# Cache attention: key products in two 512-column halves, scores of four pages at once on four column groups

## What is computed

```python
def scores(c, kr):                                    # c (128, 256), kr (128, 64)
    k = mla_keys(c, kr, w_kb, k_norm_g)               # rmsnorm(concat(c @ w_kb, kr)) per head, 8 x (128 + 64)
    return einsum('bqhe,blhe->bhql', q, k) * scale
# page_step: sc = scores(lat_pool[phys], rope_pool[phys]); online softmax; acc += pr @ c
```

## Time and profile before

| | us |
|---|---|
| median of 3 runs | 2947.7 (2947.0 to 2960.29) |
| span of the profiled execution | 2949.8 |
| PE busy (share of the span) | 2693.6 (91%) |
| PE weight loads busy | 2462.7 (83%) |
| DVE busy | 1872.8 (63%) |
| ACT busy | 1352.8 (46%) |
| POOL busy | 841.2 (29%) |
| key products L1213, three groups of 1536 | 519.5 + 497.1 + 496.6 busy |
| mean granted TensorE clock | 0.957 of 2.4 GHz |

### The profile page before, as it was taken

One profiled execution on the slowest core, in us unless ns is written; L12 is line 12 of the kernel. 1 busy time (PEld: TensorE's weight loads), 2 busy tenths in 40 slices (PEclk: granted clock), 3 DMA queues, 4 the chain that ended last, 5 costly groups with the idle time before them and its releaser, 6 DMA issues. The chain is left out here.

```text
span 2949.8 us, 62087 instructions
## 1 busy us (share of the span) xinstructions
PE 2693.6 (91%) x24092; PEld 2462.7 (83%) x24092; DVE 1872.8 (63%) x3117; ACT 1352.8 (46%) x2294; POOL 841.2 (29%) x696
## 2 busy tenths in 40 slices
PE   7987889999999899899989878799999998998998
PEld 6876459999989689899978764599999895998998
DVE  4854457777766655489448454577777676554893
ACT  4733354545444244354357333555554442533542
POOL 0030009999910400000000300199999004000000
PEclk9999989999998999999989999899999998999999
DMA  5423459677545376365453243696866344764544
GB/s 134 110 59 105 138 100 148 117 129 122 83 79 161 97 202 168 104 166 139 126 115 101 65 132 112 115 141 115 139 106 104 74 141 124 199 172 108 161 133 120
DMA packets 838374, 365.86 MB, mean 124 GB/s; under 512 B 406189, under 2 KB 825558, under 8 KB 837512
## 3 DMA queue, kind: packets, MB, share of 16 engines
q1 hardware_dynamic: 835858, 360.77, 53.7%
q10 hardware_dynamic: 2232, 1.26, 0.2%
HBM read 342.63 MB, written 61.23 MB: 137 GB/s over the span
## 5 line engine op out<-in xcount | busy, mean ns | idle before, releaser
L1213 PE MATMUL key_banks<-w_kb_head,latent_T_head 128*128 128x352 f32 x1536 | 519.5, 338 | 9.7 <-DVE latent_T_rest L1341 9.7
L1213 PE MATMUL key_banks<-w_kb_head,latent_T_rest 128*128 128x352 f32 x1536 | 497.1, 324 | 0.0
L1213 PE MATMUL key_banks<-w_kb_rest,latent_T_head 128*128 128x352 f32 x1536 | 496.6, 323 | 0.0
L297 DVE TENSOR_TENSOR w_rests<-w_ring,w_heads 128x2048 fp32r<-128x2048 f32 (+1 forms) x150 | 321.6, 2147 | 146.9 <-ACT w_heads L291 146.7
L1355 DVE TENSOR_REDUCE w_kb<-key_sq 128x8 f32<-128x1024 f32 x256 | 311.2, 1216 | 12.4 <-ACT key_sq L1278 7.7
L1213 PEld LDWEIGHTS key_banks<-w_kb_head,latent_T_head 128*128 128x128 f32 x1536 | 290.5, 189 | 23.5 <-DVE latent_T_rest L1341 11.6
L1213 PEld LDWEIGHTS key_banks<-w_kb_rest,latent_T_head 128*128 128x128 f32 x1536 | 290.9, 189 | 0.0
L1213 PEld LDWEIGHTS key_banks<-w_kb_head,latent_T_rest 128*128 128x128 f32 x1536 | 289.8, 189 | 0.0
L291 ACT CAST w_heads<-w_ring 128x2048 fp32r<-128x2048 f32 (+1 forms) x150 | 268.4, 1792 | 42.8 <-ACT conv_last_rows L1934 19.7
L1033 POOL TENSOR_TENSOR rwkv_state_tmp<-rwkv_state,vec 128x1024 f32<-128x1024 f32 x64 | 153.3, 2395 | 455.6 <-POOLq L232 450.7
L1265 ACT CAST latent_T_head<-turn_bank 128x256 fp32r<-128x256 f32 x256 | 95.3, 372 | 400.6 <-PE key_banks L1217 392.2
(11 more groups left out here) (597 smaller groups left out, 7006.1 us busy)
## 6 DMA issues: line engine op xcount, KB each, us to landing
w_ring<-in_ffn_w_up_dram SPq DMA_DIRECT2D x88, 512.0 KB, 5.0
page_latents<-in_cache_kv_latent_dram SPq DMA_DIRECT2D x256, 128.0 KB, 2.4
latent_blocks<-page_latents SPq DMA_DIRECT2D x256, 128.0 KB, 3.9
latents<-page_latents SPq DMA_DIRECT2D x64, 512.0 KB, 8.4
w_ring<-in_w_in_dram SPq DMA_DIRECT2D x52, 512.0 KB, 3.8
w_ring<-in_w_gate_dram SPq DMA_DIRECT2D x46, 512.0 KB, 4.0
w_ring<-in_w_in_dram SPq DMA_DIRECT2D x20, 1024.0 KB, 5.9
w_ring<-in_ffn_w_down_dram SPq DMA_DIRECT2D x32, 384.0 KB, 3.3
```

The lines of the kernel that those rows point to most:

```text
L297: ops.tensor_tensor(rests[:, slot, 0:tiles * P], ring[:, slot, 0:tiles * P], heads[:, slot, 0:tiles * P].bitcast(F32), ALU.subtract).then_ ...
L1213: last = nc.tensor.matmul(kbank[:, 3 * x + n, 0:KB], c[:, x, r * P:(r + 1) * P], w[:, r, cols], start=r == 0 and m == 0, stop=r == 1 and m ...
```

## The change

The queries leave the key products. These become 12 products of 512 columns a page into 4 PSUM banks. The latents are transposed into a ring of 8 pages in SBUF (`cT`) instead of PSUM, and `head` and `rest` read them there. For every four pages PE makes the scores with the queries as the stationary operand (32 columns), page g of the four on column group g: 8 fp32 products of 128 columns with `qa` and 4 with `qr` (24 rows in a trace). ACT copies the 128x128 result to SBUF, PE transposes it once (five pages after the first of the four), ACT copies it to `s`. Query copies (L1257, L1317, and L981 and L1012 in `mla_absorb`) fall away. `latents` becomes one buffer, loaded for sequence b at the end of the sequence itself instead of one sequence ahead.

```diff
-        lat = st.sb("latents", [P, 2, PAGES, LW])
+        lat = st.sb("latents", [P, PAGES, LW])
+        cT = st.sb("latent_T", [P, RC, KVRANK])          # RC = 8
+        sS = st.sb("query_scores", [P, 2, P])
-        kbank = st.ps("key_banks", [P, 6, BANK])
-        xbank = st.ps("turn_bank", [P, 2 * P])
+        kbank = st.ps("key_banks", [P, 4, BANK])
+        sbank = st.ps("score_banks", [P, 3, BANK])
...
                 def load_latents(b):
-                    if b >= 2:
-                        sp.wait_ge(outed, (b - 2) * GROUPS + GROUPS)
+                    if b:
+                        sp.wait_ge(outed, b * GROUPS)
...
+                def score(b, quad):
+                    if quad >= 2:
+                        pe.wait_ge(s_kept, quad - 1)
+                    for r in range(2):
+                        for g in range(QUAD):
+                            n = quad * QUAD + g
+                            nc.tensor.matmul(scores_of(quad)[32 * g:32 * g + 32, :], k.qa[:, r, b, :], cT[:, n % RC, r * P:(r + 1) * P],
+                                             start=r == 0, stop=False, skip_group_check=True)
+                    for g in range(QUAD):
+                        n = quad * QUAD + g
+                        last = nc.tensor.matmul(scores_of(quad)[32 * g:32 * g + 32, :], k.qr[:, n % 2, b, :], kpT[:, n // 2 % RK, :],
+                                                start=False, stop=True, skip_group_check=True)
+                    last.then_inc(scored, 1)
+                def turn_scores(quad):
+                    pe.wait_ge(s_kept, quad + 1)
+                    if quad:
+                        pe.wait_ge(taken, quad)
+                    nc.tensor.transpose(turned_scores, sS[:, quad % 2, :], k.col("ident")).then_inc(s_turned, 1)
...
                         pe.wait_ge(t_kept, base + (j + 1))
                         if not (is_first(b) and j < 2):
-                            pe.wait_ge(taken, base + (j - 1))
-                        for n in range(3):
+                            pe.wait_ge(squared, base + (j - 1))
+                        for n in range(2):
...
-                                    last = nc.tensor.matmul(kbank[:, 3 * x + n, 0:KB], c[:, x, r * P:(r + 1) * P], w[:, r, cols],
+                                    last = nc.tensor.matmul(kbank[:, 2 * x + n, :], c[:, x, r * P:(r + 1) * P], w[:, r, cols],
...
+                        if quad_to_turn(b, j) is not None:      # j % 4 == 1
+                            turn_scores(quad_to_turn(b, j))
+                        if j % QUAD == QUAD - 1:
+                            score(b, (base + j) // QUAD)
...
+                def head(n):
+                    act.wait_ge(turned, n + 1)
+                    if n >= 2:
+                        act.wait_ge(keyed, n - 1)
+                    nc.scalar.copy(ch[:, n % 2, :], cT[:, n % RC, :]).then_inc(headed, 1)
...
                 def turn(n):
+                    if n >= RC:
+                        dve.wait_ge(scored, (n - RC) // QUAD + 1)
-                    if n:
-                        dve.wait_ge(t_kept, n)
-                    nc.vector.transpose(xbank[:, :].rearrange("p (r t i) -> p r t i", r=2, t=4),
+                    nc.vector.transpose(cT[:, n % RC, :].rearrange("p (r t i) -> p r t i", r=2, t=4),
                                         blk[:, i, at, :, :, :].rearrange("p t r f -> p r t f")).then_inc(turned, 1)
-                def rest(b, j):
-                    nc.vector.tensor_tensor(cl[:, x, :], xbank[:, :], ch[:, x, :].bitcast(F32), ALU.subtract).then_inc(t_kept, 1)
+                def rest(n):
+                    dve.wait_ge(headed, n + 1)
+                    nc.vector.tensor_tensor(cl[:, n % 2, :], cT[:, n % RC, :], ch[:, n % 2, :].bitcast(F32), ALU.subtract).then_inc(t_kept, 1)
```

More of the change, by code:

```diff
@@ L1093, in cache_attention @@
         ss = reuse(1088, 2, PAGES, HEADS)
-        kpT = reuse(1344, 2, P)
-        top, inv, diag = (reuse(1600 + 32 * n, 1, 32)[:, 0, :] for n in range(3))
+        kpT = reuse(1344, RK, P)
+        top, inv, diag = (reuse(1856 + 32 * n, 1, 32)[:, 0, :] for n in range(3))
         diag = diag[0:32, :]
         kpe_sq = k.samT[:, 0:2, :, :].rearrange("p a b c -> p (a b c)").rearrange("p (j c) -> p j c", c=ROPE)
-        sq = st.sb("key_sq", [P, 2, KW + 32])
+        sq = st.sb("key_sq", [P, 2, KW])
         ssp = st.sb("rope_sumsq", [P, PAGES])
@@ L1131, in is_first, with scores_of, quad_to_turn @@
         def is_first(b):
-            return isinstance(b, int) and b == 0
+            return b == 0
         def is_last(b):
[L1135 to L1147, removed]
+            return b == LAST
+        def scores_of(quad):
+            return sbank[:, quad % 2, 0:P]
+        turned_scores = sbank[:, 2, 0:P]
+        def quad_to_turn(b, j):
+            return b * QUADS + j // QUAD - 1 if j % QUAD == 1 and (b or j > QUAD) else None
         with st.block() as block:
@@ L1255, in _, with keep_scores, take_scores, body @@
             def _(act):
-                def query(b, slot):
-                    nc.scalar.copy(wh[:, :, query_cols(slot)], k.qa[:, :, ds(b, 1), :].rearrange("p r o c -> p r (o c)")).then_inc(q_headed, 1)
-                def head(b, j):
-                    x = j % 2
-                    act.wait_ge(turned, b * PAGES + (j + 1))
-                    if not (is_first(b) and j < 2):
-                        act.wait_ge(scored, b * PAGES + (j - 1))
-                    nc.scalar.copy(ch[:, x, :], xbank[:, :]).then_inc(headed, 1)
-                def body(b, slot, uses):
+                def head(n):
[3 more added lines that the diff above has]
+                    nc.scalar.copy(ch[:, n % 2, :], cT[:, n % RC, :]).then_inc(headed, 1)
+                def keep_scores(quad):
+                    act.wait_ge(scored, quad + 1)
+                    if quad >= 2:
+                        act.wait_ge(s_turned, quad - 1)
+                    nc.scalar.copy(sS[:, quad % 2, :], scores_of(quad)).then_inc(s_kept, 1)
+                def take_scores(quad):
+                    b, q = quad // QUADS, quad % QUADS
+                    act.wait_ge(s_turned, quad + 1)
+                    nc.scalar.copy(s[:, b % 2, QUAD * q:QUAD * q + QUAD, :].rearrange("p j c -> p (j c)"), turned_scores).then_inc(taken, 1)
+                def body(b, slot):
                     base = b * PAGES
@@ L1293, in finish @@
                 def finish(b, slot, at):
+                    if at == TOTAL and is_last(b):
+                        take_scores(NB * QUADS - 1)
                     if at == LN:
@@ L1346, in body @@
                         x = j % 2
-                        if j + 2 < PAGES:
-                            rest(b, j + 2)
-                        elif not is_last(b):
-                            rest(b + 1, j + 2 - PAGES)
+                        if base + j + 2 < NB * PAGES:
+                            rest(base + j + 2)
                         if base + j + AHEAD < NB * PAGES:
@@ L1353, in body @@
                         dve.wait_ge(squared, base + (j + 1))
-                        f = first_key(slot)
-                        nc.vector.tensor_reduce(ss[:, slot, j, :], sq[:, x, f:f + KW].rearrange("p (h e) -> p h e", e=NOPE), AX.X, ALU.add).then_inc(summed, 1)
-                        if j == Q_AT and not is_first(b) and not is_last(b):
-                            query_rest(b + 1, 1 - slot)
+                        nc.vector.tensor_reduce(ss[:, slot, j, :], sq[:, x, :].rearrange("p (h e) -> p h e", e=NOPE), AX.X, ALU.add).then_inc(summed, 1)
                         if j - 1 in ROPE_AT:
```

104 lines of the change are left out of this document (41 added, 63 removed).

## The result

The changed kernel took 2968.01 us (median of 20 runs, 2956.09 to 2981.01), beside 2957.39 for the kernel before on the same chip: 1.0039 times its time, 95% interval 1.0029 to 1.0049. The forecast was 2946.0 between 2908 and 2976. The time lies inside that range, but a change of 4 us to the faster side had been forecast, and the kernel is some 11 us slower. The profiled execution has a span of 2960.9, 11.1 above the one before.

A forecast was written before the change was run, and what follows sets the result against it. PE was taken to bound attention; its 34 us gain would be mostly eaten by DVE's waits for POOL (54.2 against 53.86 us a sequence), leaving 4 us off the profiled 2949.8: 2946 us, range 2908 to 2976.

The forecast's parts named there:

- Key products: PE's 512-column products in attention: 213.3 ns plus a constant 13.3, so 226.7 a step and 2.72 us a page.
- in proportion: Alternative for the 512-column product step: surplus grows with the columns, 232.7 ns a step and 2.79 us a page.
- the first term: PE's gain in attention, resting on 227 ns product steps: 0.53 us per four pages, 34 us over 64 quads.
- The scores: PE's 24 score rows per four pages: 0.80 us, plus 0.09 for the slow first product behind them.
- the turn: PE's one transpose of the scores per four pages: 0.14 us at most.
- the PE gain: PE's time for four attention pages falls from 12.44 to 11.91 us, 34 us over 64 quads.
- The waits: DVE's rest, both operands in SBUF, waits for POOL's operation: 0.7 us a page on the mean, PE waiting in pages 2 to 6.
- two terms of the sum: PE's attention gain, 53.86 to 51.7 us a sequence, against DVE's waits for POOL, which bring it back to 54.2.
- Rival 1: Attention: PE stays the bound, rests meet POOL between operations or slack absorbs the waits; 2916 us, chance 0.27.
- Rival 2: Attention: DVE becomes the bound outright, rests queue behind POOL's 2.4 us operations; 2974 us, chance 0.17.
- Rival 3: Scores on PE: column groups run in series, 2.56 us per quad, adding 113 us; 3060 us, chance 0.02.
- What costs nothing: ACT's changed copies, dropped absorb query copies, transposes into SBUF and the single latents buffer: no cost, no gain in absorb.

The follow-up runs named there:

- e9: e3 with each 512-column key product cut in two (480 and 32, 448 and 64, 416 and 96, 384 and 128): 3167 us in a single execution.
- e1: Kernel before with POOL's recurrence replaced by a memset of its output: ratio 1.0008 to the kernel before.
- e2: Changed kernel with POOL's recurrence replaced by a memset of its output: ratio 0.9948 to the kernel before.
- e3: Changed kernel with a second transpose of each page into PSUM, from which head and rest read; turned scores share the score banks: ratio 0.9964 to the kernel before.
- e5: Kernel before with only the turned page moved from PSUM to SBUF, so the rest reads two SBUF operands: ratio 1.0148 to the kernel before.
- e4: Changed kernel with heads and rests made three pages ahead instead of two, in rings of three: ratio 1.0155 to the kernel before.
- e10: e3 with two idle DVE sums ahead of the copy the fold waits for, making PE idle once a sequence: ratio 1.0172 to the kernel before.

## Why the prediction was wrong

**The step that failed** is *Key products*: "a 512-column product should cost 213.3 + 13.3 = 226.7". It costs 233.3. A constant read at 288 and 352 columns was carried to 512, and e9 shows that it ends between them. 48 x 6.6 ns are 0.32 us for four pages (a quad), and 64 quads are 20 us of the 34 I counted. By themselves these 20 us would turn the forecast of 4 us faster into some 16 slower; the stages got 20 longer. The end I had kept for it (232.7, "in proportion") gave nearly the right number by a wrong law: in proportion, 256 columns would be 116.7, and they are 120.0. "Steps of 216 or 233 ns would undo the first term" is what happened. The rule of the Trainium skill that stood against my sum (TensorE: Matmul & The Clock Gate, Back-to-back issue gap) lies further off on the same side, with 215.8 for 233.3; the section gives that formula for a single product taken by itself, which I had left out, and these products each have a weight load ahead.

**The scores** were 0.89 + 0.10 for 0.80 + 0.09, the turn 0.11 for 0.14, together 0.07 us a quad, 4.5 us in all. With the step, the PE gain is 12.44 - 12.30 = 0.14 a quad by the rows and 7 us in both stages by e1 and e2 (3.5 each), not 34. The lower end that I gave for a quad, 0.1, allows this; the value that I used, 0.53, does not. That the time lies inside the range is in part the baseline's doing: the forecast was counted from the profiled 2949.8, with the 2.1 above the median left in, and the kernel before measured 2957.39 beside the changed one.

**The waits were right** in place and mechanism. A rest with both operands in SBUF lasts until POOL's operation is over, one with an operand in PSUM does not (e3, e5). The mean wait is 943 - 424 = 0.52 over all 256, and 0.6 over the 111 rests that start between 450 and 830 us (mean 1.01 us), where I took 0.7. The rests spread from 405 to 2605 ns, and no rest of a stage is longer than 428 once POOL's recurrence is over. PE alone is idle for 8.9 us between 450 and 830 us, 6.1 of them at pages 6 and 7 of the sequences (counted from 0), for the rest of page 6 and the softmax step beside page 7; I had them in pages 2 to 6. PE's loss was foreseen as 2.5 us a sequence; e2 and the changed kernel differ by 55.6 - 53.5 = 2.1, and by 14.1 a stage, against the 15 in my sum (6.1 x 2.5). So nearly the same waits stood against a gain of 3.5 instead of 17. One of the two terms of the sum was about right, the other a fifth of what I wrote.

**The rivals.** Rival 1, PE stays the bound, is what e2 and e3 show when the waits are taken away, and there too it is not 2916, since its PE sum was the same wrong one. Rival 2 ended on the right side, with the wrong cause: DVE was busy 43 to 52 of 54 to 58 us, not all through. Rival 3 is out: the column groups ran together, with 24 rows in 0.89 us.

**POOL.** It ran from 439.86 to 834.65, 394.8 us, for 382.9 before: 12 longer, forecast 15. Of the 111 rests, 83 met a POOL operation in progress, and each of them ended 0.28 us behind its end. The other 28 came between two POOL operations or less than 0.15 us before the end of one. They took 0.41 to 0.43 us, and here it was POOL's next operation that could be held up:

```profile
473.25 0.42 DVE L1355 TENSOR_TENSOR latent_T_rest<-latent_T,latent_T_head 128x256 fp32r<-128x256 f32 x1 [1.64 <-ACT latent_T_head L1276]
473.25 2.19 POOL L1037 TENSOR_TENSOR rwkv_state_tmp<-vec_sa,vec 128x1024 f32<-128x1024 f32 x1
```

The same POOL operation took 1.90 in the earlier trace rows, so it lost 0.29 here. Where the Trainium skill (SBUF — State Buffer, Who interferes with whom) has the loser blocked for the whole instruction, the trace agrees in both directions. The 12 us that POOL lost over the 111 rests are 0.1 each, less than the 0.29 here and than the 0.42 of a whole rest.

**What costs nothing** held: no wait for the latents buffer appears in the waits of the stage, and the absorb stage did not get shorter (from its first product to the sum over the new keys 12.2 and 13.9 us before, 13.0 and 12.2 now).

**Outside the stages** I had forecast no change, and 9 us were gained in this profile. The feed-forward part shows one piece, 1238.80 to 1487.10 in the kernel before and 1245.50 to 1488.50 in the changed one:

```profile
1238.80:1487.10 248.30, 229.11 (x1645) 223.73 (x1645) 172.64 (x328) 113.09 (x160) 0.00 (x0) 0.95 0.53 142
```

```profile
1245.50:1488.50 243.00, 224.35 (x1645) 219.48 (x1645) 172.71 (x328) 112.98 (x160) 0.00 (x0) 0.98 0.53 145
```

The same 1645 products, 5.3 us apart, at a mean clock of 0.95 and 0.98. Between the same two rows the other ten profiles have 243.8 to 248.0 us, on the whole longer the lower the granted clock: 248.0 at 0.95 (e1), 243.8 at 0.98 (e5). It does not go by the kernel. Why the clock falls there in one run and not in the next was not tried. The sum of the stages, +20, and the median, +11, are therefore not the same number. In e4 too the stages are 54 us longer and the median 45. That gap stays open.

## What to carry to other kernels

Before moving an operand of a frequent VectorE operation from PSUM to SBUF, look whether GpSimd works beside it: here that one move cost 14 to 21 us a stage, and a second transpose that kept one operand in PSUM paid for itself. Do not carry a step time to a width that no row shows; time it alone first. And where TensorE stands because it takes late work in its order, count the stand twice: once as time and once for the clock that may fall behind it. More depth can move such a stand to another step and make one long one of several short ones, as it did in e4.

## What was not expected of the hardware

- With a weight load ahead of each, product steps exceed their columns at 2.4 per ns by 13.3 ns at 256, 288 and 352 columns, by 17 to 20 from 384 to 480, by 20.0 at 512; from 32 to 128 columns they do not fall below 110.
- A VectorE subtraction of 256 columns with both operands in SBUF that met a GpSimd operation in progress ended 0.28 us behind that operation, 83 times of 83 in the changed kernel; with one operand in PSUM (e3, the kernel before) it took 396 to 432 ns beside the same work.
- Stands of PE of 1.9 us (e5), 2.6 (e10) and 2.7 (e4) were followed by 3.4 to 6.8 us at a granted clock of 0.50, but in e10 behind six of seven nearly equal stands of the first stage only. In e5 a stand of 1.95 us that ended at 776.4 was followed by none, and one of 1.37 at 808.4 was. The changed kernel, whose longest stand was 1.37 too, kept 1.00 behind the first page of its first stage. What decides whether the clock falls is not told by these rows.
